# Moving the weight slots, the normed columns and the arena to other SBUF offsets modulo 256 bytes in a two-block language-model kernel

## What is computed

```python
ub = u_tab[ib]
vb = v_tab[ib]
act = jax.nn.gelu(jnp.einsum('td,thkd->thk', xb, ub).astype(F32), approximate=False)
return jnp.einsum('thk,thkd->td', (gb * act).astype(vb.dtype), vb)
```

## Time and profile before

| | |
|---|---|
| median of 3 executions | 3,288.23 us (3,284.37 to 3,289.87) |
| the profiled execution, its own time | 3,285.75 us |
| span of its instructions | 3,283.9 us |
| TensorE (PE) busy | 2,854.2 us, 87% |
| weight loads (PEld) busy | 2,248.3 us, 68% |
| VectorE (DVE) busy | 2,441.1 us, 74% |
| ScalarE (ACT) busy | 771.0 us, 23% |
| GpSimd (POOL) busy | 618.8 us, 19% |
| mean granted TensorE clock | 0.940 of full |

### The profile page before, as it was taken

How to read it: one execution, slowest core, us unless ns; L and a number is a source line. 1 busy time by engine, 2 the same in 40 slices (tenths; PEclk the granted TensorE clock), 3 DMA queues, 4 the chain that set the end, 5 groups by cost and what they waited for, 6 DMA issues and landing times. The chain is left out here.

```text
span 3283.9 us, 44518 instructions
## 1 busy us (share of the span) xinstructions
PE 2854.2 (87%) x17520; PEld 2248.3 (68%) x17520; DVE 2441.1 (74%) x4651; ACT 771.0 (23%) x1993; POOL 618.8 (19%) x520
## 2 busy tenths in 40 slices
PE   8999987777777889877777777999998999998899
PEld 8889853333333789533333325999887999997898
DVE  7455687777776886877777767878747878877786
ACT  4322222222222343222222222011323001023300
POOL 0000034444444100344444441000000000000000
PEclk9999998888998999988888888999999999999899
DMA  6454699999999637899999996665204666652464
GB/s 211 147 172 155 212 377 419 416 410 419 408 402 421 230 104 237 341 419 417 419 415 399 407 421 253 195 202 162 68 28 154 192 204 185 207 184 87 135 195 148
DMA packets 471089, 868.24 MB, mean 264 GB/s; under 512 B 18912, under 2 KB 399712, under 8 KB 403168
## 3 DMA queue, kind: packets, MB, share of 16 engines
q0 software_dynamic: 73728, 536.90, 39.6%
q1 hardware_dynamic: 396864, 328.24, 31.6%
q10 hardware_dynamic: 288, 0.24, 0.0%
HBM read 855.89 MB, written 9.44 MB: 264 GB/s over the span
## 5 line engine op out<-in xcount | busy, mean ns | idle before, releaser
L2834 PE MATMUL banks<-arena,arena 128*128 128x512 f32 x1744 | 911.6, 681 | 315.7 <-ACT arena L2911 315.7
L2834 PEld LDWEIGHTS banks<-arena,arena 128*128 128x128 f32 x1744 | 370.4, 219 | 838.5 <-issue 448.9
L2792 POOL DMA_INDIRECT arena<-in_peer_uv,arena x512 | 613.8, 1199 | 1310.9 <-PE banks L2834 636.5
L3069 DVE CUSTOM_DVE_ANT_0 arena<-arena,normed 128x1024 f32<-128x1024 f32 x512 | 625.8, 1223 | 226.8 <-DMA arena<-in_peer_uv,arena 224.2
L457 DVE TENSOR_TENSOR weight_ring_part<-weight_ring,weight_high_parts 128x2048 fp32r<-128x2048 f32 (+3 forms) x243 | 537.6, 2212 | 8.3
L3623 PE MATMUL banks<-normed_columns_part,weight_high_parts 128*128 128x256 f32 x1408 | 394.1, 280 | 2.9 <-DVE weight_ring_part L457 2.4
L3624 PE MATMUL banks<-normed_part,weight_high_parts 128*128 128x256 f32 x1408 | 391.8, 278 | 0.0
L3625 PE MATMUL banks<-normed_columns_part,weight_ring_part 128*128 128x256 f32 x1408 | 391.6, 278 | 0.0
L454 DVE CAST weight_high_parts<-weight_ring 128x2048 fp32r<-128x2048 f32 (+3 forms) x243 | 288.6, 1188 | 92.6 <-PE banks L930 64.9
L928 PE MATMUL banks<-weight_high_parts,arena_part 128*128 128x256 f32 x1200 | 337.3, 281 | 7.0 <-PEq L397 3.9
L929 PE MATMUL banks<-weight_ring_part,arena_part 128*128 128x256 f32 x1200 | 334.1, 278 | 0.0
(11 more groups left out here) (606 smaller groups left out, 4265.9 us busy)
## 6 DMA issues: line engine op xcount, KB each, us to landing
weight_ring<-in_ffn_w_gate SPq DMA_DIRECT2D x88, 512.0 KB, 3.7
weight_ring<-in_ffn_w_up SPq DMA_DIRECT2D x88, 512.0 KB, 4.9
weight_ring<-in_ev_w_in SPq DMA_DIRECT2D x33, 1024.0 KB, 5.5
weight_ring<-in_ffn_w_down SPq DMA_DIRECT2D x32, 1024.0 KB, 5.2
weight_ring<-in_od_w_in SPq DMA_DIRECT2D x23, 1024.0 KB, 5.3
weight_ring<-in_peer_wq SPq DMA_DIRECT2D x16, 1024.0 KB, 5.6
weight_ring<-in_xa_wkv SPq DMA_DIRECT2D x13, 1024.0 KB, 5.7
weight_ring<-in_ev_w_out SPq DMA_DIRECT2D x12, 1024.0 KB, 5.4
```

What stands on the lines that cost most here:

```text
L2792: pool.indirect_dma_start(out=ring[:, slot(i, s), :], out_offset=None, in_=table, in_offset=bass.IndirectOffsetOnAxis(ap=index[:, i % 2, s ...
L2834: mm = pe.matmul(k.ps[:, 2 * b + half, :], diag[:, g % 2, s, :], v, start=n == b * PEER_TOPK, stop=n == last_mixed[b])
L3069: dve.tensor_tensor_reduce(out=ring[:, here, 0:D], in0=ring[:, here, 0:D], in1=k.xn[:, i % NB, :], scale=1.0, scalar=0.0, op0=ALU.mult, op ...
```

## The change

Three edits, all of place:

- a slot of both weight rings loses its 32 spare floats (`SLOT`), so all slots begin at the same offset modulo 256;
- `tile` no longer adds 128 bytes by parity, so a tile begins where its slot does, streamed or loaded;
- 16 unused floats (64 bytes) are put ahead of `normed`.

`weight_ring` and `weight_high_parts` give up 768 bytes in all, and 64 come back ahead of `normed`. `constants` to `norm_scale_columns` move by -768 bytes, which is 0 modulo 256; `normed`, `normed_columns` and `arena` move by -704, which is +64. Modulo 256 all weight tiles then lie at 128, and `normed`, `normed_columns` and `arena` at 0. No instruction, wait or transfer is added, taken away or moved.

```diff
-SLOT = KC * WIDTH + LINE
+SLOT = KC * WIDTH
...
         self.wide = sb("norm_scale_columns", [P, T])
+        sb("line_rest", [P, LINE // 2])
         self.xn = sb("normed", [P, NB, D])
...
     def tile(self, buffer, slot, n):
         kc, width = self.plan[n][0].shape[1], sum(src.shape[2] for src in self.plan[n])
-        at = LINE * ((slot + (0 if n in self.streamed else 1)) % 2)
-        return buffer[:, slot, at:at + kc * width].rearrange("p (c n) -> p c n", c=kc)
+        return buffer[:, slot, 0:kc * width].rearrange("p (c n) -> p c n", c=kc)
```

## The result

The changed kernel takes 3,311.62 us (median of six executions, 3,310.24 to 3,314.36). The kernel before, run beside it, takes 3,292.47 us (3,284.37 to 3,297.65). The ratio is 1.0062, 95% interval 1.0051 to 1.0074: 19 us slower. The profiled execution of after took 3,311.77 us with a span of 3,309.9 us, against 3,285.75 and 3,283.9 us. This execution of before is one of its quick ones, 6.7 us under the median of the six, so the two traces differ by 26.0 us where the medians differ by 19. I had forecast 3,270 us and faster; the time lies in the range, on its other side.

What follows compares the result with a forecast made beforehand. Gathers were taken to bound the PEER stages and TensorE the rest; the short step throughout saves 18.0 us, from 3,285.75 to 3,267.8 us profiled, plus 2.5 us for the median, so 3,270 us (chance 0.28), range 3,248 to 3,319.

Steps and rivals of the forecast that it cites:

- What bounds the kernel: Gathers set the pace in the two PEER stages (413 and 414 GB/s); TensorE sets it outside them.
- The step at distance 128: Split products outside the PEER stages: 113.3 ns for every matmul, in place of a mix of 113.3 and 117.8.
- a still longer step: Rival for the split products: a step longer than any seen, from 120 ns on, ending above 3,325 us; chance 0.07.
- the four seams: Where line 3625's stream meets line 928's load at distance 0; the step switches there, taken as sign that distance matters.
- How much reaches the end: Outside PEER stages: 2,503 long steps in eight always-busy stretches whole, 2,044 others by three quarters, 4.45 ns each: 18.0 us.
- VectorE and plain float32: VectorE's splits unchanged (2,292 ns at 0, 2,293 at 128); plain float32 matmuls in PEER's mixing, 429 ns, nothing to gain.
- Faster gathers: Rival in the PEER stages: rows landing at 0 instead of 192 save 13 us per cent; about 3,258 us, chance 0.04.
- Weight transfers: Loaded tiles landing at 128 instead of 0: no cost, as 1 KB packets take 0.0031 of DMA share per GB/s at both.
- Nothing: Rival for the split products: load and stream don't meet, the mix of steps stays; 3,288 us, chance 0.26.
- The slow pace everywhere: Rival for the split products: 117.8 ns becomes the only step, costing 25.6 us; 3,314 us, chance 0.22.
- The load's bound: Rival for the split products: load and stream never meet, 111.7 ns for all, 33.8 us gained; 3,254 us, chance 0.13.
- Slower: Whole kernel slower by over 0.2%: slow pace everywhere 0.22 plus the longer step 0.07, chance 0.29.

Runs made afterwards that it cites:

- before moved: Kernel before with 64 unused bytes ahead of its first tensor, every large tensor 64 bytes further, distance still 192, gathers at 0: 3,280.08 us, ratio 0.9967.
- before with its gathers at 0: Kernel before with 16 floats skipped ahead of the gathered rows' ring, so rows land at 0 instead of 192 modulo 256: 3,275.02 us, ratio 0.9943.
- after with its gathers at 64: Changed kernel with 16 floats skipped ahead of the gathered rows' ring, so rows land at 64 instead of 0: 3,324.01 us, ratio 1.0089 to before.
- after moved: Changed kernel with 64 unused bytes ahead of its first tensor, distance still 128, gathers at 64: 3,325.60 us, ratio 1.0101 to before.
- the floats alone: Kernel before plus only the 64 bytes ahead of normed, slots and parity kept; columns and arena at 0: 3,315.14 us, ratio 1.0070.

## Why the prediction was wrong, point by point

**What bounds the kernel: right.** Where TensorE is always busy, sums of steps and measured delays agree within 0.5 us in each of seven stretches (the table above). In the PEER stages the end did not move later with the longer step.

**The step at distance 128: the term that failed.** I took 113.3 ns, "the commoner of the two states seen, and nearer to the load's own bound". It is 118.7 or 120.0. The fault lay in the bounds: I took the long step of before, 117.8, for the upper end "for every matmul", and at nine of the fourteen distances tried the mean is above it; only the rival "a still longer step" went beyond, at 0.07. All rows at hand had the distance 192, but for the pairs at the four seams. That pair said that distance matters, as I wrote, and nothing of which way. 192 happens to be the best of the fourteen, so a move to any other of them could only lose; a sample taken at one distance could not tell me that.

**How much reaches the end: nearly right.** The prediction's own rule (always-busy stretches whole, the rest by three quarters) with the measured step of 118.9 gives 5,763 x 5.6 + 4,036 x 1.1 ns = 36.7 us. (One of the eight stretches that it calls always busy was not quite so: 58.78 of 59.00 us, from 3214.) Measured were 36.6 us with the gathers at 0 in both kernels (31.5 beside before moved) and 30.2 with them off 256 in both; the executions of before beside the latter spread over 17 us, so I make nothing of the 5 to 6 us between. Matched matmul by matmul, after ends 36.6 us behind before with its gathers at 0: 8.1 us of it by 2,005 us, 28.5 later. So most of what is given back by 2,005 us is the gathers' doing. From 0 to 404 us, where nothing is gathered, it can't be, and there the longer steps (5.1 us) did not show at the end (0.3 us earlier). The granted clock is 0.99 there, against 0.98 before, for the same 2,656 records. First after, then before, over this stretch and over one of its places:

```profile
0.00:405.00 405.00, 386.82 (x2656) 0.99 0.56 179
363.00:367.00 4.00, 4.00 (x20) 1.00 0.86 270
```

```profile
0.00:405.00 405.00, 385.26 (x2656) 0.98 0.55 179
363.00:367.00 4.00, 4.00 (x13) 0.57 0.42 132
```

Set side by side, the two traces show what made it up. The clock stands at its lower level for 10.2 us from 52.7 us and for 3.4 us from 363.3 us before, and only for 6.8 us from 56.0 us after; that gives back 2.0 and 1.7 us. The third part is a wait of TensorE for VectorE's line 2447 near 360 us, 2.84 us long before and 0.76 us after, into which 2 us of longer steps went. Nothing ties the clock's part to the change: the traces of after with its gathers at 64 and of after moved have the same 13.7 us at the lower level as before.

**VectorE and plain float32: right.** 2,292 ns as before. Weight transfers and the gathers' landing place are another matter.

**Faster gathers, held at 0.04: came true, beside the rest.** I let decide: packets of 1 KB cost 0.0031 of a share per GB/s at 0 as at 128, "both are 0.0031", and so I took nothing for any packet. The rows were right and the wrong ones: they are of another size. Packets of 8,192 bytes gained 1.5%. My price was 13 us for each per cent of the 1,300 us, so 1.5% is 19.5 us; measured were 18.7 and 12.4, and 12.4 again in before moved.

**Weight transfers, taken at nothing: wrong in kind, and it cost nothing.** The gate and up tiles come in packets of 512 bytes. At 0 one takes 27.7 ns, at 128 and at 64 29.8 ns, 7.6% more, and at 192 30.3 ns. The windows had it: 0.67 / 185 = 0.0036 of a share per GB/s from 2050 us after, for 0.67 / 197 = 0.0034 before. By the same section of the Trainium skill it would be, as an estimate, 20 beats for 16 at 128, 25%; the trace shows less than a third of that, and for 1 KB nothing where the same count gives an eighth. The page's DMA issues of after (median us to landing last; 3.7 and 4.9 before) show the tiles later:

```profile
weight_ring<-in_ffn_w_gate SPq DMA_DIRECT2D x88, 512.0 KB, 4.0
weight_ring<-in_ffn_w_up SPq DMA_DIRECT2D x88, 512.0 KB, 5.3
```

TensorE never waited for them in these stretches, where it is busy for every microsecond.

**The rivals.** "Nothing" (0.26) is refuted: the mix of steps did not stay. The section "A bandwidth-pool intuition that's wrong (but worth ruling out)" of the Trainium skill's "SBUF — State Buffer", with its second, independent read port for LDWEIGHTS, spoke for it. The page says nothing of placement; that placement is then worth nothing was my reading, and the trace disagrees with it for these products, since moving one operand by 64 bytes (the floats alone) takes the step from 113.3 or 117.8 to between 118.7 and 120.0. "The slow pace everywhere" (0.22, 3,314 us) is 2 us from the measured time, but by luck: it had the step at 117.8 and no gain from the gathers, and the two errors cancel. In 2043.5 to 2140 it wanted 822 records, and there were 815. The load's bound was reached by no distance; the nearest is 113.3 at 192.

**Chances.** "Slower" had 0.29 and happened. Given one sampled distance, an even spread over the possible steps would have been nearer to what I knew than a first place for the best one.

## What to carry to other kernels

When a placement decides a rate, bounds read at one placement are no bounds for another: sweep the offset (five or six builds that differ in one number of unused floats) before arguing which is good. In products like these, whose weight load is nearly as long as their stream, keep the distance of streamed and loaded operand modulo 256 at what the sweep shows, here 192. Let large gathered rows land on multiples of 256 bytes, and judge each transfer by packets of its own size.

## What the runs showed of the hardware that I had not expected

- The step of a float32r matmul of 256 columns, whose load alone allows 111.7 ns, takes values from 113.3 to about 121.5 ns by the distance of its operands modulo 256 bytes, the same with the two swapped. The distance of 128, half way round, is among the slow ones (118.7 or 120.0), and 0 (120.0) is no worse than 96.
- At one distance there can be more than one step, each held for hundreds of matmuls: 113.3 and 117.8 ns at 192 and 64, 118.7 and 120.0 at 128, 117.3 and 118.7 at 160, and three at 56. What picks one at a restart, why 64 falls nearly always into the longer one and 192 in about half to most of the stretches into the shorter, and why only these two distances allow 113.3 at all, stays open: no run here tells it. The kernel before alone spread from 3,284 to 3,303 us over its executions; that the mix of the two steps does this was only argued.
- Of the write side of a transfer: 8,192-byte packets take 309.2 ns on 256 bytes and 313.9 ns at 64 and at 192; 512-byte packets 27.7 ns at 0 and 29.8 to 30.3 ns at 64, 128 and 192; 1 KB packets the same at 0 and at 128.
